# A chunked recurrence whose triangular inverse is taken as two diagonal blocks of 64 instead of one of 128

## The reference

```
def rwkv7_scan(r, w, k, v, kk, a):
    # S_t = S_{t-1} diag(w_t) - (S_{t-1} kk_t)(kk_t * a_t)^T + v_t k_t^T ;  y_t = S_t r_t
    def step(state, inp):
        r_t, w_t, k_t, v_t, kk_t, a_t = inp
        sa = jnp.einsum('bhvk,bhk->bhv', state, -kk_t)
        state = (state * w_t[:, :, None, :] + sa[..., None] * (kk_t * a_t)[:, :, None, :]
                 + v_t[..., None] * k_t[:, :, None, :])
        return state, jnp.einsum('bhvk,bhk->bhv', state, r_t)
    _, y = lax.scan(step, jnp.zeros((B, H, N, N), f32), xs)
```

## Time and profile before

| | |
|---|---|
| median of 3 runs | 4008.1 us (4007.0 to 4009.63) |
| profiled execution, span from its first to its last instruction | 4008.1 us |
| mean granted TensorE clock | 0.934 of full speed |
| TensorE busy | 3480.4 us (87%) |
| VectorE busy | 1688.1 us (42%) |
| the recurrence, layer 0 | from 698.3 us, the next stage's first product at 944.8 us |
| the recurrence, layer 1 | from 1730.7 us, as long |

### The profile page before, as it was taken

One profiled execution on the slowest core, in us unless ns is written; L12 is line 12 of the kernel. 1 busy time (PEld: TensorE's weight loads), 2 busy tenths in 40 slices (PEclk: granted clock), 3 DMA queues, 4 the chain that ended last, 5 costly groups with the idle time before them and its releaser, 6 DMA issues. The chain is left out here.

```text
span 4008.1 us, 38008 instructions
## 1 busy us (share of the span) xinstructions
PE 3480.4 (87%) x13936; PEld 1752.2 (44%) x13937; DVE 1688.1 (42%) x3091; ACT 701.3 (17%) x1412; POOL 196.3 (5%) x263
## 2 busy tenths in 40 slices
PE   8998999888899999889889977778699978788775
PEld 4454434885444444378634432223243344422222
DVE  3235556775232555567548420000238766200002
ACT  1132204000112330310010100000122243100001
POOL 0001010001000001000000000000100130000000
PEclk9999999999999999899889989999889989799998
DMA  3115452004121226200143099999533421799996
GB/s 105 68 48 209 143 169 60 1 1 144 47 89 32 68 83 208 55 11 1 59 175 122 0 396 429 428 428 399 202 105 121 110 73 62 310 429 419 429 428 283
DMA packets 208086, 696.40 MB, mean 174 GB/s; under 512 B 22248, under 2 KB 105704, under 8 KB 182608
## 3 DMA queue, kind: packets, MB, share of 16 engines
q1 hardware_dynamic: 178576, 589.56, 38.4%
q0 software_dynamic: 29376, 105.05, 7.2%
HBM read 636.28 MB, written 58.28 MB: 173 GB/s over the span
## 5 line engine op out<-in xcount | busy, mean ns | idle before, releaser
L345 PE MATMUL bank<-fm,w 128*128 128x512 f32 (+1 forms) x912 | 397.3, 596 | 11.4 <-DMA w<-in_ab_w_in 6.3
L2796 PE MATMUL bank<-experts_wu,experts_hs 128*64 128x512 f32 x1120 | 275.8, 650 | 75.0 <-DMA experts_wu<-in_moe_w_up 75.0
L2796 PE MATMUL bank<-experts_wg,experts_hs 128*64 128x512 f32 x1120 | 272.2, 642 | 60.1 <-DMA experts_wg<-in_moe_w_gate 45.6
L345 PE MATMUL bank<-w,fm 128*128 128x512 f32 (+2 forms) x768 | 315.5, 567 | 6.5 <-DMA w<-in_w_in 6.5
L2861 DVE TENSOR_TENSOR fm<-bank,fm 128x512 f32<-128x512 f32 x35 | 37.0, 1056 | 638.9 <-PE bank L2796 638.9
L2796 PE MATMUL bank<-experts_wd,fm 128*64 128x512 f32 x1120 | 256.4, 611 | 45.4 <-issue 24.0
L345 PEld LDWEIGHTS bank<-fm,w 128*128 128x128 f32 (+1 forms) x912 | 172.4, 190 | 234.1 <-issue 221.0
L726 PE MATMUL bank<-fm,side_w 128*128 128x512 f32 x512 | 252.4, 619 | 6.9 <-DMA side_w<-in_w_in 5.4
L345 PEld LDWEIGHTS bank<-w,fm 128*128 128x128 f32 x768 | 142.2, 195 | 179.2 <-issue 153.8
L2796 PEld LDWEIGHTS bank<-experts_wu,experts_hs 128*64 128x64 f32 x1120 | 85.9, 148 | 263.2 <-issue 166.1
L2796 PEld LDWEIGHTS bank<-experts_wg,experts_hs 128*64 128x64 f32 x1120 | 94.6, 147 | 233.6 <-issue 230.5
(11 more groups left out here) (484 smaller groups left out, 4875.5 us busy)
## 6 DMA issues: line engine op xcount, KB each, us to landing
experts_wg<-in_moe_w_gate SPq DMA_DIRECT2D x64, 2048.0 KB, 19.5
experts_wu<-in_moe_w_up SPq DMA_DIRECT2D x64, 2048.0 KB
experts_wd<-in_moe_w_down SPq DMA_DIRECT2D x64, 2048.0 KB
ada_w<-in_ada_w POOLq DMA_DIRECT2D x96, 512.0 KB, 4.9
w<-in_w_in SPq DMA_DIRECT2D x40, 512.0 KB, 3.9
expert_rows<-fm POOLq DMA_DIRECT2D x35, 512.0 KB, 10.3
fm<-expert_rows SPq DMA_DIRECT2D x33, 512.0 KB, 21.6
w<-in_w_in SPq DMA_DIRECT2D x16, 1024.0 KB, 7.2
```

Of the source, the lines that this page charges most:

```text
L345: ins = pe.matmul(bank, lhsT, rhs, start=(n == 0), stop=(n == len(todo) - 1))
L2796: ins = pe.matmul(bank[rows, :], lhs[:, k, rows], weights[:, s, k, cols], start=(k == 0), stop=(k == chunks - 1))
```

## The change

The triangle of 128 tokens is cut into its two diagonal blocks of 64 tokens and the 64 x 64 corner between them. The two blocks are inverted side by side: a tile `[P, 4, HALF]` holds the first block in partitions 0 to 63 and the second in partitions 64 to 127, and `each` issues a product of 64 x 64 by 64 x 64 for either half, with the result in the same partitions of the same bank. The first half thus uses rows 0 to 63 and columns 0 to 63 of the array, the second rows and columns 64 to 127. Both still use blocks of 16 inside, but now F^4 is zero, so the step f4 and one product of the squarings' kind go away. X is turned by a product with the identity, instead of a transpose. The scores lose one of their four matrices (384 columns instead of 512), since A and its transpose are computed again as 64 x 64 blocks (`p_halves`), the transpose's corner with them. The corner is multiplied by the second block's inverse beside the step w (L1668), and one new step, carry, subtracts the corner's product with the first half of the update from the second half. There are 14 steps instead of 15, and 28 rounds a chunk instead of 30.

```diff
-        G = [sb(f"G{s}", [P, 4, 4, P]) for s in range(2)]
-        M, Q, E, X = ([sb(f"{n}{s}", [P, 4, P]) for s in range(2)] for n in ("M", "Q", "E", "X"))
-        M2, Q2 = ([sb(f"{n}{s}", [P, 4, P]) for s in range(2)] for n in ("M2", "Q2"))
+        G = [sb(f"G{s}", [P, 4, 3, P]) for s in range(2)]
+        powers, powers2 = ([sb(f"{n}{s}", [P, 2, 4, HALF]) for s in range(2)] for n in ("powers", "powers2"))
+        E, X, corner = ([sb(f"{n}{s}", [P, 4, HALF]) for s in range(2)] for n in ("E", "X", "corner"))
...
-            def each(pe, bank, lhsT, rhs):
+            def each(pe, bank, n, lhsT, rhs):
                 for i in range(4):
-                    last = pe.matmul(bank[:, i * P:(i + 1) * P], lhsT[s][:, i, :], rhs[s][:, i, :], start=True, stop=True)
+                    cols = slice((4 * n + i) * HALF, (4 * n + i + 1) * HALF)
+                    for rows in (first, second):
+                        last = pe.matmul(bank[rows, cols], lhsT[rows, i, :], rhs[rows, i, :], start=True, stop=True)
                 return last
...
-            def p_turned(pe, b):
+            def p_halves(pe, b):
                 for i, h in enumerate(heads):
-                    last = pe.matmul(b[h % 2][:, (i // 2) * P:(i // 2 + 1) * P], right[half(h), h // 2, 0, tok],
-                                     left[half(h), h // 2, 0, tok], start=True, stop=True)
+                    at = [slice(t * P + a * HALF, t * P + (a + 1) * HALF) for a in range(2)]
+                    l, r = ([m[half(h), h // 2, 0, at[a]] for a in range(2)] for m in (left, right))
+                    upper_at, lower_at, corner_at = (slice((2 * n + i // 2) * HALF, (2 * n + i // 2 + 1) * HALF) for n in range(3))
+                    for a, rows in enumerate((first, second)):
+                        pe.matmul(b[i % 2][rows, upper_at], l[a], r[a], start=True, stop=True)
+                        pe.matmul(b[i % 2][rows, lower_at], r[a], l[a], start=True, stop=True)
+                    last = pe.matmul(b[i % 2][second, corner_at], r[1], l[0], start=True, stop=True)
...
+            def p_square(pe, b):
+                each(pe, b[0], 0, lower(powers), upper(powers))
+                return each(pe, b[0], 1, upper(powers), lower(powers))
+            yield p_square, lambda dve, link, b: dve.tensor_copy(powers2[s][:, :, :, :], both_sets(b[0]))
+
+            def p_fourth(pe, b):
+                each(pe, b[0], 0, lower(powers2), upper(powers2))
+                each(pe, b[0], 1, upper(powers2), lower(powers2))
+                return each(pe, b[1], 0, lower(powers2), X[s])
...
             def p_w(pe, b):
...
+                for i in range(4):
+                    last = pe.matmul(b[1][first, i * HALF:(i + 1) * HALF], corner[s][second, i, :], X[s][second, i, :],
+                                     start=True, stop=True)
                 return last
...
             def p_u(pe, b):
+                return each(pe, b[0], 0, X[s], neg_w[s])
...
+            def p_carry(pe, b):
                 for i in range(4):
-                    last = pe.matmul(b[0][:, i * HD:(i + 1) * HD], X[s][:, i, :], neg_w[s][:, i, :], start=True, stop=True)
+                    last = pe.matmul(b[0][second, i * HD:(i + 1) * HD], corner[s][first, i, :], upd[s][first, i, :], start=True, stop=True)
                 return last
...
+            def e_carry(dve, link, b):
+                return dve.tensor_tensor(upd[s][second, :, :], upd[s][second, :, :], one_set(b[0])[second], ALU.subtract)
```

More of the change, by code:

```diff
@@ L51 @@
 NCH = SEQ // CH
+HALF = CH // 2
 SUB = 16
@@ L1571, in p_turned, with e_halves @@
                 return last
-            def e_turned(dve, link, b):
+            def e_halves(dve, link, b):
                 for o in range(2):
[L1575 to L1593, removed]
-                    last = dve.tensor_copy(q2[s][:, :, :], all_heads(b[1]))
-                    if update:
-                        last = dve.tensor_tensor(X[s][:, :, :], X[s][:, :, :], all_heads(b[2]), ALU.add)
-                    return last
-                return p, e
@@ L1599, in phases @@
-            yield square(M, Q, M2, Q2, False, False)
-            yield square(M2, Q2, M, Q, True, False)
-            yield square(M, Q, M2, Q2, True, True)
-            def p_last(pe, b):
-                return each(pe, b[0], Q2, X)
-            def e_add(dve, link, b):
-                return dve.tensor_tensor(X[s][:, :, :], X[s][:, :, :], all_heads(b[0]), ALU.add)
-            yield p_last, e_add
+                    sets = b[o][:, 0:6 * HALF].rearrange("p (n a t) -> p n a t", n=3, a=2)
+                    dve.tensor_tensor(powers[s][:, :, o::2, :], sets[:, 0:2], over(chip.sub_masks, [P, 2, 2, HALF], 2), ALU.mult)
@@ new lines, in e_halves, with add_to_x @@
+                    dve.tensor_tensor(E[s][:, o::2, :], sets[:, 0], over(chip.off_upper, [P, 2, HALF], 1), ALU.mult)
+                    last = dve.tensor_scalar(corner[s][second, o::2, :], sets[second, 2], SCORE_SCALE, None, ALU.mult)
+                link(last)
+                return dve.tensor_tensor(X[s][:, :, :], over(chip.half_ident, [P, 4, HALF], 1), upper(powers), ALU.subtract)
+            yield p_halves, e_halves
+            def add_to_x(dve, bank, op=ALU.add):
+                return dve.tensor_tensor(X[s][:, :, :], X[s][:, :, :], one_set(bank), op)
@@ new lines, in e_fourth, with p_eighth, e_eighth @@
+            def e_fourth(dve, link, b):
+                dve.tensor_copy(powers[s][:, :, :, :], both_sets(b[0]))
+                return add_to_x(dve, b[1])
+            yield p_fourth, e_fourth
+            def p_eighth(pe, b):
+                each(pe, b[0], 0, upper(powers), lower(powers))
+                return each(pe, b[1], 0, lower(powers), X[s])
+            def e_eighth(dve, link, b):
+                dve.tensor_copy(lower(powers2), one_set(b[0]))
+                return add_to_x(dve, b[1])
@@ L1611, in p_xt @@
+            yield p_eighth, e_eighth
+            yield (lambda pe, b: each(pe, b[0], 0, lower(powers2), X[s])), lambda dve, link, b: add_to_x(dve, b[0])
             def p_xt(pe, b):
                 for i in range(4):
-                    last = pe.transpose(b[0][:, i * P:(i + 1) * P], X[s][:, i, :], chip.ident)
+                    for rows in (first, second):
+                        last = pe.matmul(b[0][rows, i * HALF:(i + 1) * HALF], X[s][rows, i, :], chip.ident[rows, rows], start=True, stop=True)
@@ L3130, in shape_constants @@
     same = (row // CH) == (col // CH)
-    sub = (row // SUB) == (col // SUB)
+    part_row, part_col = row % HALF, np.arange(HALF)[None, :]
+    sub = (part_row // SUB) == (part_col // SUB)
     strict, incl = same & (row < col), same & (row <= col)
```

80 lines of the change are left out of this document (39 added, 41 removed).

## The result

| | median | against the kernel before on the same chip |
|---|---|---|
| before | 4007.55 us (3996.29 to 4009.63, 4 runs) | |
| after | 3878.07 us (3873.85 to 3888.52, 4 runs) | 0.9684, 95% interval [0.966, 0.9707] |

The change makes the kernel 3.2% faster, 129.5 us by the medians. The forecast was 3886 us, 8 us away. The profiled execution of the changed kernel has a span of 3886.8 us, 121.3 less than the 4008.1 before.

A forecast was written before the change was run, and what follows sets the result against it. Most of a chunk was taken as bound by TensorE. Steps of 36.0 us plus clock 3.0, normalization 2.0, array-form changes 1.0 and rest 1.4 gave 43.4 us a chunk, 122 us saved, 3886 us; range 3858 to 3975.

The forecast's parts named there:

- price of the quarters: In products of `each`: sixteen quarter instructions run in pairs and take 0.45 us, against 0.89 one by one.
- The additions: Per-chunk costs beyond the summed steps: clock 3.0, normalization and output 2.0, array-form changes 1.0, the rest 1.4 us.
- Rival B: In `each`, quarters take turns because different row halves write one bank: 0.89 us an `each`, 3971 us; chance 0.13.
- C's slower products: Quarter instructions come slower, an `each` of 0.6 us; with C's low-clock alternative, 3930 to 3948 us; chance 0.13.
- Mode changes and the rest: Across a chunk: switching between half, quarter and full array, 1.0 us more, plus 1.4 us the step sum missed.
- the rule: Per pair of rounds, the larger of both streams' products and products + 0.31 + evacuation + 0.05; 36.0 us a chunk.
- Normalization: VectorE's normalization and output of the chunk before, 5.4 us in three of four chunks; half shows, 2.0 us.
- The clock: Time lost to the half clock after the change, put at 3.0 us a chunk.
- the same low activity at the chunk's start: The reason given for the 3.0 us clock addition: low activity at the scores stays, seen by more of the stage.
- What was to be seen: Signs in the trace: chunks of 41 to 46 us, granted clock 0.85 to 0.94, sixteen instructions every 0.45 us.
- TensorE's idle time before L1557: Idle time before the `each` products, ended by VectorE, expected at some 10 us a chunk.
- Rival D: Idle gaps between rounds and half-filled array keep the clock at 1.2 GHz from halves through y; 4065 us; chance 0.08.

The follow-up runs named there:

- scores4: The changed kernel with the scores' fourth matrix restored, evacuations of 512 instead of 384 columns; 3903.7 us, ratio 0.9756.
- no_norm: The changed kernel without normalization and output of each layer's first three chunks; no valid total, chunks sum to 312.2 us.
- same_rows: The changed kernel with both products of a pair reading rows 0 to 63, second block's inverse left out; chunks sum to 426.5 us, total not comparable.
- late_out: The changed kernel with the previous chunk's output step moved from round 22 to behind round 26; 3853.6 us, ratio 0.9628.
- y_early: The changed kernel with y's update-independent products issued behind u and carry, losing part of y; chunks sum to 320.6 us, total not comparable.
- norm_late: late_out's idea with the previous chunk's normalization pieces in rounds 15 to 21, transposes at 24, output step at 27; 3859.8 us, ratio 0.9648.

## Why the prediction was right

The mechanism and the price of the quarters were right, and the sum holds by its steps at full clock. The additions were mis-sized in opposite directions, one of them for a wrong reason, and that the total still came so near is in part luck. The first chunk, from the starts in its timeline:

| step | predicted | measured |
|---|---|---|
| scores and halves (to 707.25) | 7.2 | 7.7 |
| square (to 710.69) | 2.9 | 3.4 |
| fourth (to 714.22) | 3.1 | 3.5 |
| eighth, last (to 718.26) | 3.7 | 4.0 |
| xt (to 719.47) | 1.2 | 1.2 |
| f (to 721.37) | 1.95 | 1.9 |
| f2, last (to 724.91) | 3.2 | 3.5 |
| w, u, carry (to 731.81) | 6.0 | 6.9 |
| y (to 738.26) | 6.2 | 6.45 |

f2 is taken without the output transposes, which the first chunk lacks: 35.5 predicted, 38.7 measured.

- **The price of the quarters** decided the forecast. 0.45 us for sixteen was taken and 0.465 measured. Rival B is refuted by the same rows: two row halves write one bank in pairs, at 0.465 where B needs 0.9. The Trainium skill's rule (TensorEngine Tiling (Array Packing), Restrictions and Gotchas), by which different row tiles cannot use one bank at the same time, does not hold in this trace, where their PSUM partitions differ. C's slower products did not come either.
- **Mode changes and the rest**, 1.0 + 1.4: the measured excess of the first chunk over the rule is 3.2. It is spread over nearly all steps. The four short ones with an `each` (last twice, u, carry) have some 1.3 of it, at 1.4 to 1.6 instead of 1.2. How much of it is changes of the array's form was not measured.
- **Normalization** 2.0 as a mean over the chunks: 1.65 in six of eight, 1.24. (Its VectorE work is ten instructions and 5.3 us, not eleven and 5.4.)
- **The clock**, 3.0 a chunk: the size was near, the reason wrong. The step that failed is "the same low activity at the chunk's start". There the changed kernel keeps 1.00 in its first chunk, because VectorE's evacuation of the scores got shorter (scores4 brings the low clock back), and 3.4 us of low clock are left in three others. Most of it went to carry and y instead, behind a wait for the output step that the sum didn't name, and it took more as the layer went on. That the size came out near is luck. Twice (1 - clock) times the length gives 0, 3, 7 and 13 us at the low clock in the first four chunks, where the kernel before has 7 in most. Taken as what is left, it costs 352.54/8 - 38.74 - 1.24 = 4.1 us a chunk.
- Together: 44.1 us a chunk measured against 43.4, 120.7 us saved in the stage against 122. The two agree better than their parts, and that is luck as well: the 58.6 us of a chunk before is a mean of four, and all eight give 473.22/8 = 59.15. Both sides of the difference were some 0.6 us too short.
- **What was to be seen**: chunks of 41 to 46 us is true of four of eight, and a clock of 0.85 to 0.94 of four. TensorE's idle time before L1557, put at 10 us a chunk, is far less: the whole chunk has 4.5 us of idle time in the first (38.74 - 34.21) and 5.9 in the third.
- **Rival D** was named for the right reason: idle time can bring the clock down, and it did, for 8 us a chunk instead of the whole stage. The guess that the gaps between short steps would do it was wrong (no_norm, which has the same gaps and 3.4 us of low clock in three of eight chunks).

## What to carry to other kernels

Two products on diagonal quarters of the array run together, also into one PSUM bank, when they are issued in turn; a block-diagonal matrix is worth treating as such. After a change that makes TensorE's part short, look in the clock column at what stands ahead of the stretch where TensorE still bounds: here 0.9 us of idle time, put there by a VectorE step of other work, cost 24 us, and moving that step was one number. And where data decides how much work a later stage has, an experiment that changes the values is to be read by its own stage, not by its total.

## What the runs showed of the hardware

- Sixteen instructions of 64 x 64 float32 products, on the two diagonal quarters in turn, take 0.465 us, 29 ns each; with shared rows and separate columns the same; with the four products of a half in a row some 0.68; and eight of one quarter alone take as long as sixteen in turn.
- TensorE busy 43.95 of 44.30 us was granted 0.50 when the products of `each` used 64 of the 128 rows, where the same instructions over both row halves kept 1.00 (same_rows against the changed kernel's first chunk; the values differ too, since the second products read other data). Being busy was not enough to get the full clock back. Neither was it in the changed kernel's fourth chunk, where y's products use all rows and TensorE was busy for 13.24 of 13.24 us at 0.50.
- The clock fell behind TensorE's waits for VectorE at three places (the scores, carry, and the output step ahead of the scores). For the first two, a shorter wait kept it up (after against scores4; late_out and y_early against after); the third came with a longer one (norm_late against late_out), in two chunks of four.
